# Splitting ten SBUF buffers between gathered rows and dense tiles: six and four in place of five and five

## What is computed

```
def chunk(zc):                                   # 128 tokens
    ... top_k over two key sets -> expert (8 heads x 16), gate = softmax(top_s)
    u = jnp.take(peer_u, expert, axis=0)         # 16384 experts, rows of 2048
    act = jax.nn.gelu(jnp.einsum('chkd,cd->chk', u, zc))
    v = jnp.take(peer_v, expert, axis=0)
    w = gate * act
    return jnp.einsum('chk,chkd->cd', w, v)
```

## Time and profile before

| | us |
|---|---|
| median of three runs | 2656.57 |
| lowest, highest | 2652.78, 2658.17 |
| the profiled execution, its own time | 2660.49 |
| its span | 2658.7 |

### The profile page before, as it was taken

One profiled execution on the slowest core, in us unless ns is written; L12 is line 12 of the kernel. 1 busy time (PEld: TensorE's weight loads), 2 busy tenths in 40 slices (PEclk: granted clock), 3 DMA queues, 4 the chain that ended last, 5 costly groups with the idle time before them and its releaser, 6 DMA issues.

```text
span 2658.7 us, 32188 instructions
## 1 busy us (share of the span) xinstructions
PE 2244.7 (84%) x11476; PEld 1810.2 (68%) x11476; DVE 2102.6 (79%) x2954; ACT 1140.5 (43%) x1717; POOL 665.5 (25%) x854
## 2 busy tenths in 40 slices
PE   8999999999999999989999953444555558999997
PEld 7997778888888888879988831111223226777776
DVE  6986647665566656567866999999999989899997
ACT  5433555443344344453642111000455534548876
POOL 1000000000000000000302354433434442886663
PEclk9999999999999999999999976566677778999999
DMA  6534354555555655545568999999999995999996
GB/s 227 184 125 110 111 159 158 189 190 184 186 186 187 188 189 185 155 150 174 179 211 355 421 419 419 420 419 420 419 419 408 420 419 173 368 393 409 409 407 266
DMA packets 314517, 732.02 MB, mean 275 GB/s; under 512 B 21040, under 2 KB 223024, under 8 KB 275760
## 3 DMA queue, kind: packets, MB, share of 16 engines
q0 software_dynamic: 73728, 402.69, 37.3%
q1 hardware_dynamic: 240544, 327.03, 36.4%
q10 hardware_dynamic: 144, 1.05, 0.1%
HBM read 728.61 MB, written 2.10 MB: 275 GB/s over the span
## 4 chain that ended last, share of the span: by engine, by line
DVE 20%; DMA 17%; PE 16%; issue 3%; POOL 1%; ACT 1%; DVEq 0%; ACTq 0%; PEldq 0%
DVE row L2545 11%; DMA row<-in_peer_v_rows,expert 8%; DMA row<-in_peer_u,expert 8%; PE pl L887 4%; PE pl L894 4%; DVE pl L2561 3%; PE pg L1313 2%; PE pl L890 2%; PE pl L891 2%; PE pl L1278 1%; PE pg L1304 1%; POOL row L823 1%; DMA v_tile<-in_peer_v_dense 1%; PE pl L1207 1%; DVE hot_b L2585 1%
## 5 line engine op out<-in xcount | busy, mean ns | idle before, releaser
L1987 DVE TENSOR_TENSOR wlo<-raw,whi 128x1024 fp32r<-128x1024 f32 (+1 forms) x436 | 519.6, 1211 | 362.9 <-ACT whi L1360 361.1
L1360 ACT ACTIVATE whi<-raw 128x1024 fp32r<-128x1024 f32 (+1 forms) x436 | 445.1, 1039 | 415.6 <-PE pl L894 411.3
L2545 DVE CUSTOM_DVE_ANT_0 row<-row,pg 128x2048 f32<-128x2048 f32 x256 | 574.6, 2283 | 34.1 <-DMA row<-in_peer_u,expert 31.3
L1278 PE MATMUL pl<-row,diag 128*128 128x512 f32 x404 | 313.3, 921 | 335.5 <-DMA row<-in_peer_v_rows,expert 299.5
L887 PE MATMUL pl<-x_split,whi 128*128 128x512 f32 x1888 | 476.4, 394 | 5.2 <-DVE x_split L2145 3.8
L1278 PEld LDWEIGHTS pl<-row,diag 128*128 128x128 f32 x404 | 100.6, 275 | 499.5 <-issue 430.9
L887 PEld LDWEIGHTS pl<-x_split,whi 128*128 128x128 f32 x1888 | 340.7, 190 | 68.2 <-issue 3.1
L894 PE MATMUL pl<-x_split,wlo 128*128 128x256 f32 x2656 | 372.8, 283 | 0.0
L894 PEld LDWEIGHTS pl<-x_split,wlo 128*128 128x128 f32 x2656 | 358.2, 192 | 18.8 <-DVE wlo L1987 0.2
L823 POOL DMA_INDIRECT row<-in_peer_u,expert x256 | 242.1, 946 | 369.6 <-DVE dots L2545 159.3
L823 POOL DMA_INDIRECT row<-in_peer_v_rows,expert x256 | 267.6, 1045 | 200.5 <-DVE dots L2545 65.3
(11 more groups left out here) (347 smaller groups left out, 3060.8 us busy)
## 6 DMA issues: line engine op xcount, KB each, us to landing
v_tile<-in_peer_v_dense SPq DMA_DIRECT2D x128, 512.0 KB
raw<-in_w_in SPq DMA_DIRECT2D x51, 1024.0 KB
raw<-in_w_gate SPq DMA_DIRECT2D x44, 1024.0 KB
raw<-in_w_up SPq DMA_DIRECT2D x44, 1024.0 KB
raw<-in_w_out SPq DMA_DIRECT2D x32, 1024.0 KB
raw<-in_w_down SPq DMA_DIRECT2D x32, 1024.0 KB
wq<-in_peer_wq SPq DMA_DIRECT2D x15, 1024.0 KB, 11.4
raw<-in_w_down SPq DMA_DIRECT2D x16, 768.0 KB
```

The costliest lines, as they stand in the source:

```text
L1278: last = mm(pl_all[:, c:c + width], diag[:, (at - 1) % 4, :], row[b][:, c - DENSE:c - DENSE + width], start=at == 1, stop=at == ADDED_ROWS ...
L1360: return nc.scalar.activation(o, i, ACT.Copy)
L1987: V.tensor_tensor(wlo[:, n % 4, 0:k, :], w[:, :, f, :], whi[:, n % 4, 0:k, :].bitcast(F32), ALU.subtract)\
L2545: V.tensor_tensor_reduce(row[b][:], row[b][:], z_tok[:], 1.0, 0.0, ALU.mult, ALU.add, dots[:, at:at + 1])\
```

## The change

Rows from position `LATER` on rotate through six buffers. The sixth, row 23, lies at `("arena", 2 * D)`, where tile home 0 was and, earlier, row buffer 3; its first gather waits for the last user of that buffer (`ROWS_FROM`). Dense tiles rotate through four homes, which are the former homes 1 to 4, and signal by `slot_full`. The second home now lies where `hot_a` and `hot_b` are, so SP's wait for the weight matrix stands before tile 1 and not before tile 2. Nothing is computed otherwise, and the number of instructions is the same on every engine.

```diff
--- before.py
+++ after.py
@@ -97,12 +97,12 @@
 ADDED_END = PRODUCTS + ADDED_ROWS
 SUMMED_ROWS = PRODUCTS - ADDED_ROWS
 ROWS_AT = {0: range(2), 2: range(2, 4), 8: range(4, 6), 20: range(6, 7), 24: range(7, 9), 31: range(9, 11), 37: range(11, 13),
-           43: range(13, 17), SCATTERED: range(17, 18), LATER: range(18, 23)}
+           43: range(13, 17), SCATTERED: range(17, 18), LATER: range(18, 24)}
 ROWS_LEFT = {SCATTERED: (4, 5, 6, 7, 8, 11, 12, 13, 14), LATER: range(18)}
 ROWS_FREE = {2: 1, 8: 2, 20: 4, 24: 5, 31: 6, 37: 7, 43: PH}
-ROWS_ALL = 23
-ROWS_FROM = {}
-ROWS_SIGNAL = [*range(18), *ROWS_LEFT[SCATTERED][0:5]]
+ROWS_ALL = 24
+ROWS_FROM = {23: 3}
+ROWS_SIGNAL = [*range(18), *ROWS_LEFT[SCATTERED][0:6]]
 
 
 def row_buffers():
@@ -152,7 +152,7 @@
 
 
 RING = 4
-TILE_HOMES = RING + 1
+TILE_HOMES = RING
 HIGHS = 3
 UNIT = 2048
 KU = 8
@@ -333,7 +333,7 @@
         homes += [("whi", 0), ("whi", D), ("wlo", 0), ("xlo", 0), ("xlo", D), ("wlo", D), ring[1]]
         homes += [ring[2], ring[3], ("mix", 0), ("mix", D), ("tmp", 0)]
         row = [sb(f"row{n}", region, start, [P, D]) for n, (region, start) in enumerate(homes)]
-        homes = [*(("xhi", m * GATHERED) for m in range(4)), ("arena", 3 * D)]
+        homes = [*(("xhi", m * GATHERED) for m in range(4)), ("arena", 3 * D), ("arena", 2 * D)]
         row += [sb(f"row{len(row) + n}", region, start, [P, GATHERED]) for n, (region, start) in enumerate(homes)]
 
 
@@ -345,8 +345,7 @@
         HOTS = len(hot_homes)
         spread_all = sb("spread_all", "raw", 0, [P, TT, 5 * 16 * S])
         spread = [spread_all[:, t, 0:NKEY * P].rearrange("p (i c) -> p i c", i=NKEY) for t in range(TT)]
-        tile_homes = [("arena", 2 * D), ("arena", 3 * D + DENSE), ("arena", 4 * D), ("arena", 4 * D + DENSE),
-                      ("rest", choice_at)]
+        tile_homes = [("arena", 3 * D + DENSE), ("arena", 4 * D), ("arena", 4 * D + DENSE), ("rest", choice_at)]
         high_homes = [("arena", 2 * D + DENSE), ("rest", choice_at + DENSE), ("rest", choice_at + 2 * DENSE)]
         v_tile = [sb(f"v_tile{m}", region, start, [P, DENSE]) for m, (region, start) in enumerate(tile_homes)]
         v_lo = [sb(f"v_lo{m}", region, start, [P, DENSE], F32R) for m, (region, start) in enumerate(tile_homes)]
@@ -504,7 +503,7 @@
         hot_ready = sem("hot_ready")
         hot_used = sem("hot_used")
         spread_ready = sem("spread_ready")
-        tile_full = [*slot_full, x_in[0]]
+        tile_full = slot_full
         tile_hi, tile_lo = w_hi, w_lo
         spread_high, spread_low = x_hi, x_lo
         tile_used = sem("tile_used")
@@ -536,7 +535,7 @@
         def tile_landed(m):
 
             n = m % TILE_HOMES
-            earlier = max(LOADS[u] for u in range(len(LOADS)) if u % RING == n) if n < RING else 1
+            earlier = max(LOADS[u] for u in range(len(LOADS)) if u % RING == n)
             return 16 * (earlier + m // TILE_HOMES + 1)
 
         def sq_count(n, t4):
@@ -688,7 +687,7 @@
             sp.wait_ge(dot_done, PRODUCTS)
             sp.wait_ge(row_added, EARLY)
             for m in range(NKEY):
-                if m == 2:
+                if m == 1:
 
                     sp.wait_ge(hot_used, TT * GROUPS)
                     sp.wait_ge(row_added, ADDED_ROWS)
```

## The result

| | us |
|---|---|
| before, median of 4 runs (lowest to highest) | 2656.27 (2652.78 to 2658.17) |
| changed, median of 4 runs | 2685.34 (2684.16 to 2692.12) |
| ratio, 95% interval | 1.0120 (1.0108 to 1.0132) |
| the profiled execution, own time and span | 2684.16, 2682.3 |

The forecast was 2659.6 us, range 2651 to 2670. The time lies 29 us above before and 15 us above the range. It is what rival 1 described (the tile ring decides), at three times its price.

The account below looks back on a forecast made before the run. The prediction took VectorE to bound the first 40 dense tiles and DMA the other 88. Terms 1 + 0 + 2 + 0 = +3 us on the profiled 2660.49 gave 2663.5, or 2659.6 us on the runs' scale, range 2651 to 2670.

Parts of the forecast that it names:

- rival 1: Tile ring, tile 40 on: loads stay at 6.75 us with ten transfers outstanding; 9.3 us slower, 2666 us; chance 0.25.
- What bounds the kernel before: Dense stretch: VectorE sets the first 40 tiles' pace (3.06 us), DMA the other 88 (2.96 us), TensorE close behind.
- One tile read ahead, +1: Start of the dense stretch: tile 1's load waits for the weight matrix; +1 us, ends 0 and 3.5.
- Tiles 0 to 39 with four homes, 0: Turn of 11.3 us over four homes is 2.82 us a tile, under VectorE's 3.06; 0 us.
- Tiles 40 to 127, +2 taken from 0 to 8: Turn of 12.2 us over four homes is 3.05 us a tile against 2.96; +8 unless loads shorten, +2 taken.
- The rule of turns between queues: By it a tile's load depends only on tiles ahead, shortening with four homes; later tiles' term 0 rather than 8.
- The sixth row buffer, 0: Row ring: POOL's 45.5 us of buffer waits shorten, but DMA limits the gain; ends 0 and -2.3, 0 taken.
- Rival 2: POOL's order: later tiles hold `low_weights` and gathers behind it, 32 places; +13 us, 2670 us; chance 0.12.
- Rival 3: Dense stretch: DMA not at its limit, a fuller gather queue reaches 419 GB/s; 7.7 us faster, 2649 us; chance 0.08.
- theory T: Set up for the experiments: a tile home's turn (load, rounding, copy, subtraction, matmuls) over four homes sets the pace.

Follow-up runs that it names:

- experiment 4: Kernel before with a sixth tile home from tile 13 on, five row buffers kept: 2656.58 us, ratio 1.0004.
- experiment 6: Kernel before with each tile home given back four matmuls sooner: 2656.14 us, ratio 1.0002.
- experiment 12: Five row buffers, a sixth tile home from tile 14 on, homes given back after the eight matmuls that read them: 2657.68 us, ratio 1.0006 to the kernel before.
- experiment 11: Kernel before with each of the 155 summed gathers fetching 512 columns and not 1024: 2642.40 us, ratio 0.9945.
- experiment 2: Kernel before with one tile read ahead and not two, five row buffers and five tile homes kept: 2658.68 us, ratio 1.0011.
- experiment 3: Changed kernel with a fifth tile home from tile 12 on, six row buffers kept: 2658.70 us, ratio 1.0019 to the kernel before.
- experiment 1: Changed kernel with five row buffers again, four tile homes and one tile read ahead: 2692.51 us, ratio 1.0139 to the kernel before.
- experiments 9: Changed kernel with each of the 155 summed gathers fetching 512 columns and not 1024: 2658.36 us, ratio 1.0011 to the kernel before.
- 10: Changed kernel with each of the 155 summed gathers fetching only 16 columns: 2645.50 us, ratio 0.9962 to the kernel before.

## Why the prediction was wrong, step by step

- **What bounds the kernel before:** right, as far as one ring at a time can tell. Experiments 4, 6 and 12 loosen the tile ring and gain nothing; experiment 11 takes bytes away and gains 13 us until TensorE is full.
- **One tile read ahead, +1:** right as far as the runs can tell. The trace shows +1.0 us by tile 40 in experiment 2, and by tile 4 the changed kernel had caught up (its `v_lo` 16.95 us after that of tile 0, before 16.7). The runs of experiment 2 give +0.3 to +5.6.
- **Tiles 0 to 39 with four homes, 0:** off by some 3 us of the +4.0, for the same reason as the next term. The sum of 11.3 us left a cover of 0.24 us a tile, and it counted no wait. Followed through the trace (tiles 10 to 39), the turn is 12.45 us, 3.11 us a tile, which is the pace of that stretch. Between the start of `v_hi` and that of `v_lo` lie 2.00 us and not 1.06, since VectorE is busy with rows.
- **Tiles 40 to 127, +2 taken from 0 to 8:** this is the step that failed; it measured +23.7. The turn over four homes was set at 12.2 us and is 12.98. The sum is right for a turn that meets no busy engine (the piece of 12.28 us above). It put at nothing what a turn waits for on the way:

| part of the turn, us | prediction | trace, mean of tiles 40 to 123 |
|---|---|---|
| load, issue to landing | 6.75 | 6.53 |
| landing to start of `v_hi` | 0 | 0.19 |
| start of `v_hi` to start of the copy | 1.28 | 1.34 |
| start of the copy to start of `v_lo` | 1.07 | 1.23 |
| `v_lo` | 1.2 | 1.22 |
| end of `v_lo` to the first matmul that reads it | 0 | 0.33 |
| eight matmuls, first start to last end | 1.9 | 2.09 |
| to the next load's issue | 0 | 0.04 |
| turn | 12.2 | 12.98 |

What is missing are the waits for an engine that is still busy (0.19 us for ScalarE, 0.16 for VectorE before `v_lo`, 0.33 for TensorE) and 0.19 us in the eight matmuls. (The piece of 12.28 us has some hundredths of each wait too: 0.08 us from landing to `v_hi`, 0.05 from `v_lo` to TensorE.) The matmuls were counted at 0.235 us each, which is the distance from one to the next in a stream; from the first's start to the last's end they take 2.02 us in a stream and 2.12 us behind a wait (medians). The missing 0.78 us are 0.19 us a tile, 17 us over 88 tiles, on top of the 8 that were the upper end.

The second, smaller part of the error, 6 us, is that I took +2 and not +8, by the argument that a load "need come only 0.4 us sooner" and that "with one tile fewer outstanding it should". Beside the 6.75 us of the sum a load came 0.2 us sooner, half of what was needed. The medians, from kernel to kernel, say 0.4 (2400 to 2600 us, us from issue to landing; the trace of before lacks part of the landings, so experiment 2 stands for five and five):

| rows, tiles | tile's load | gather |
|---|---|---|
| 5, 5 (experiment 2) | 6.9 | 9.5 |
| 6, 5 (experiment 3) | 7.1 | 10.1 |
| 6, 4 (changed) | 6.5 | 7.1 |
| 5, 4 (experiment 1) | 6.7 | 7.3 |

The rows of experiment 2 and of experiment 1, for 2400 to 2600 us:

```profile
v_tile<-in_peer_v_dense SPq DMA_DIRECT2D x68, 512.0 KB, 6.9
row<-in_peer_v_rows,expert POOLq DMA_INDIRECT x87, 9.5
```

```profile
v_tile<-in_peer_v_dense SPq DMA_DIRECT2D x59, 512.0 KB, 6.7
row<-in_peer_v_rows,expert POOLq DMA_INDIRECT x77, 7.3
```

With four homes a gather landed 2.2 to 3.0 us sooner and a tile 0.4. Number times median over 200 us gives, as an estimate, how many were in flight: 4.1 gathers in experiment 2 and 2.8 with the change, although there were six buffers for them. So the DMA had fewer transfers to carry, and moved less (376 GB/s after 405), and still a tile's load came down by 0.4 us only. Even the full 0.4 us wouldn't have been enough, since the turn around the load was longer than I had set it.

- **The rule of turns between queues.** The Trainium skill ("DMA: Bandwidth & Descriptors", Queues, rings and completion order) says that a DMA engine takes turns between the queues that have work. The table agrees as far as it goes: a tile's load hardly depends on how many gathers are in flight (4.1 or 2.8), and experiments 9 and 10 show that it does depend on the gathers' bytes. What I made of it, that the term would be 0, was wrong: with one tile fewer the load shortened by 0.4 us, and the turn is made of more than the load. Why the load shortens so little is not shown.
- **The sixth row buffer, 0:** right. POOL's waits for a buffer went away and nothing was gained (experiment 3 against experiment 2).
- **Rival 1:** right mechanism, priced at +9.3, measured +29. Its price rested on the same turn of 12.2 us. Its reason, that ten outstanding transfers fill the DMA as before, didn't come true: fewer were in flight and the loads were no longer than before. **Rival 2** (POOL's order): its sign came, POOL's waits for `spread_hi` went from 29.8 to 79.1 us, but VectorE's waits for rows fell to 0.4 us. Experiment 3 has 65.1 us of that wait with five homes, where nothing is lost, so by itself it costs nothing: POOL waits for `spread_hi` once it no longer waits for a buffer. **Rival 3:** GB/s fell, and experiments 3 and 4 stay at 404.

## What to carry to other kernels

When a ring of buffers gets shorter, add up its whole turn and divide by the new number. The bare durations give only a turn that waits for nobody (12.2 to 12.3 us here); add what a turn waits for where an engine has other work in between (0.7 us here), and take a group of matmuls from its first start to its last end. If the result lands above the pace, every hundredth of a microsecond counts once per tile. Take the load from all tiles and not from the chain, which picks the late ones (6.5 us, where the changed kernel's chain suggested 7.3 and theory T went by it). Don't count on the load getting shorter: beside another queue's gathers it lost 0.4 us when one tile fewer could be in flight. Waits that vanish on one ring (45.5 and 14.3 us here) say nothing if the DMA or another ring sets the pace: only widening one ring at a time showed which did.

## What the runs showed that I had not expected

- A DMA share near 1 is no sign of a DMA at its limit: 1.02 goes with 405 GB/s, 0.99 with 376 and 0.97 with 365 (experiment 1), all in 2400 to 2630 us with the same kind of packets.
- A gather on 64 of 128 partitions slowed packets from 155 to 249 ns in its own queue and from 154 to 233 ns in the other, so that half the gathered bytes made the kernel 63 us slower than the changed one.
